# Even block of a two-part transformer: shorter mixing of attention pairs, norm in pieces, cosine products on GpSimd, keys and values of the second softmax later

## The reference, cut to what matters

```python
def diff_attention(q, k, v, lam, subln, lambda_init):      # 4 heads, each a pair of softmaxes
    s = einsum('bqhcd,bkhcd->bhcqk', q, k) * scale
    p = masked_softmax(s, mask)                            # chunk-causal mask
    w = p[:, :, 0] - lam * p[:, :, 1]                      # the pair is mixed
    o = einsum('bhqk,bkhe->bqhe', w, v)                    # 128 values for each head
    return rmsnorm(o, subln) * (1.0 - lambda_init)         # norm over each head's 128 values

def dsa_attention(q, k, v, qi, ki, wi, topk):              # 8 heads of 64
    score = sum over 8 index heads of relu(qi @ ki) * wi
    keep the 64 best keys of each row                      # topk = 64
    p = softmax of q @ k * scale over these; return p @ v

even_mixer = concat(diff_attention, dsa_attention) @ w_out # q and k of both get rotary embedding
```

## Time and profile before

| what | us |
|---|---|
| median of three runs | 1515.05 (1514.8 to 1518.71) |
| the profiled execution, its own time | 1513.2 |
| its span in the trace | 1511.4 |
| TensorE busy in the span | 1441.9 (95%) |
| VectorE busy | 923.5 (61%) |
| ScalarE busy | 746.5 (49%) |
| GpSimd busy | 77.6 (5%) |

### The profile page before, as it was taken

How to read it: one execution, slowest core, us unless ns; L and a number is a source line. 1 busy time by engine, 2 the same in 40 slices (tenths; PEclk the granted TensorE clock), 3 DMA queues, 4 the chain that set the end, 5 groups by cost and what they waited for, 6 DMA issues and landing times.

```text
span 1511.4 us, 17972 instructions
## 1 busy us (share of the span) xinstructions
PE 1441.9 (95%) x6775; PEld 1179.4 (78%) x6775; DVE 923.5 (61%) x1118; ACT 746.5 (49%) x1019; POOL 77.6 (5%) x129
## 2 busy tenths in 40 slices
PE   5999998999999999999889999999999999999998
PEld 4878876778877888877667888878888777778886
DVE  5587775778776554477946655456554555665543
ACT  4556735646546444355446534445344455564442
POOL 3011100000000000031000000000000100000000
PEclk9999999999999999998889999999999999999999
DMA  9786645467554655353214755538555463366550
GB/s 353 271 301 217 205 149 162 166 234 244 191 167 153 223 195 182 129 181 112 100 39 154 263 183 195 187 106 266 180 194 190 124 195 112 112 228 203 195 167 29
DMA packets 177446, 274.29 MB, mean 181 GB/s; under 512 B 6449, under 2 KB 120881, under 8 KB 177361
## 3 DMA queue, kind: packets, MB, share of 16 engines
q1 hardware_dynamic: 170656, 250.87, 49.7%
q0 software_dynamic: 5552, 20.20, 4.3%
q10 hardware_dynamic: 1153, 2.07, 0.4%
HBM read 272.05 MB, written 1.06 MB: 181 GB/s over the span
## 4 chain that ended last, share of the span: by engine, by line
PE 66%; DVE 9%; issue 3%; ACT 2%; DMA 2%; POOL 0%; SPq 0%; DVEq 0%; POOLq 0%; ACTq 0%
PE psum L2189 20%; PE psum L2191 20%; PE psum L2190 20%; DVE w_lo L1810 3%; DMA raw<-in_w_up_dram 2%; DVE PR L2128 2%; PE psum L2390 2%; ACT w_hi L1616 1%; PE psum L2319 1%; PE psum L2318 1%; PE psum L2265 1%; DVE scr L2151 1%; PE psum L2334 1%; DVE lo_at L1810 1%; PE psum L2280 0%
## 5 line engine op out<-in xcount | busy, mean ns | idle before, releaser
L1810 DVE TENSOR_TENSOR w_lo<-raw,w_hi 128x2048 fp32r<-128x2048 f32 (+1 forms) x158 | 358.6, 2273 | 183.6 <-ACT w_hi L1616 183.0
L2189 PE MATMUL psum<-w_hi,hT_hi 128*128 128x512 f32 x1000 | 403.4, 403 | 18.9 <-DVE w_lo L1810 8.5
L2191 PE MATMUL psum<-w_hi,hT_lo 128*128 128x512 f32 x1000 | 393.1, 393 | 0.0
L2190 PE MATMUL psum<-w_lo,hT_hi 128*128 128x512 f32 x1000 | 392.9, 393 | 0.0
L1616 ACT ACTIVATE w_hi<-raw 128x2048 fp32r<-128x2048 f32 (+1 forms) x158 | 299.6, 1899 | 136.7 <-PE psum L2191 91.8
L2189 PEld LDWEIGHTS psum<-w_hi,hT_hi 128*128 128x128 f32 x1000 | 190.8, 191 | 67.4 <-issue 20.9
L2191 PEld LDWEIGHTS psum<-w_hi,hT_lo 128*128 128x128 f32 x1000 | 190.1, 190 | 41.1
L2190 PEld LDWEIGHTS psum<-w_lo,hT_hi 128*128 128x128 f32 x1000 | 190.7, 191 | 37.1 <-issue 0.5
L1810 DVE TENSOR_TENSOR lo_qk<-raw,hi_qk 128x2048 fp32r<-128x2048 f32 (+1 forms) x35 | 79.2, 2264 | 41.2 <-ACT hi_qk L1616 41.2
L2189 PE MATMUL psum<-w_hi,hc_hi 128*128 128x512 f32 x256 | 100.5, 393 | 1.8 <-DVE hc_lo L1815 1.1
L1810 DVE TENSOR_TENSOR lo_at<-raw,hi_at 128x2048 fp32r<-128x2048 f32 x35 | 80.1, 2290 | 35.8 <-ACT hi_at L1616 35.8
(11 more groups left out here) (210 smaller groups left out, 2064.2 us busy)
## 6 DMA issues: line engine op xcount, KB each, us to landing
raw<-in_ffn_wg_dram SPq DMA_DIRECT2D x88, 512.0 KB, 3.7
raw<-in_ffn_wu_dram SPq DMA_DIRECT2D x88, 512.0 KB, 4.7
raw<-in_ffn_wd_dram SPq DMA_DIRECT2D x44, 1024.0 KB, 4.9
raw<-in_w_up_dram SPq DMA_DIRECT2D x44, 512.0 KB, 5.1
raw<-in_w_in_dram SPq DMA_DIRECT2D x19, 1024.0 KB, 7.4
ada_raw<-in_w_ada_dram POOLq DMA_DIRECT2D x24, 512.0 KB, 5.1
raw<-in_even_w_in_dram SPq DMA_DIRECT2D x12, 1024.0 KB, 5.0
raw<-in_odd_w_in_dram SPq DMA_DIRECT2D x12, 1024.0 KB, 5.2
```

Of the source, the lines that this page charges most:

```text
L1810: nc.vector.tensor_tensor(lo_of(s), raw_of(s), hi_of(s).bitcast(F32), ALU.subtract).then_inc(lo_ready, 1)
L2189: nc.tensor.matmul(o, a_hi, b_hi, start=start, stop=False)
L2190: nc.tensor.matmul(o, a_hi, b_lo, start=False, stop=False)
L2191: return nc.tensor.matmul(o, a_lo, b_hi, start=False, stop=stop)
```

## The change

Five things are done in the even block.

1. **Mixing.** Before, both probabilities of a pair were scaled (two operations each) and added. Now the second alone is scaled, by lambda times the first's sum over the second's sum, and added to the unscaled first. The factor that is left, one over the first's sum, is applied to the output in `diffout`.
2. **diffout** works in pieces of one head: for each of 2 row tiles and 4 heads a scaled square with its sum (128 columns), and a scaled copy. That is 16 operations of ScalarE in place of 4.
3. **Norm in pieces.** The sums of squares on VectorE are gone. `diffvar` (one small operation) stands in step 1 of the second softmax, `diffnorm` is four operations of 128 columns for a row tile, one tile in step 2 and one in step 3.
4. **Cosine products on GpSimd** for `bq` and `bk`: four products of 128x512 on GpSimd for each, and VectorE only adds.
5. **Fillers moved.** `first_of(4)` and `second_of` go from steps 3, 4 to steps 5, 6, the rotary embedding of `bk` from step 5 to step 7, `fill_turn` of `bq` from 5 to 4; the projection of the values, `first_of(5)` and `second_of`, goes from steps 6, 8 of the first softmax to steps 0, 1 of the second; `turn_first` and `out_first` stand one step earlier.

```diff
             fills = [[first_of(3), topk(0)], [second_of, topk(1)], [topk(2), rope_of(3, "bq")],
-                     [first_of(4), topk(3)], [second_of, topk(4)],
-                     [fill_turn(3, "bq", 8), topk(5), rope_of(4, "bk")],
-                     [topk(6), first_of(5)], [topk(7)], [second_of], [fill_turn(4, "bk", 12)]]
+                     [topk(3)], [fill_turn(3, "bq", 8), topk(4)],
+                     [first_of(4), topk(5)],
+                     [second_of, topk(6)], [topk(7), rope_of(4, "bk")], [], [fill_turn(4, "bk", 12)]]
...
-            fills = [[], [lambda: pl.add("diffnorm", uses=o_diff, st=sd, v=v, n=sd["n"])], [], [], [],
-                     [turn_first("scr", ("scr_ready", v))], [out_first(W["even_w_out"][0])]]
+            fills = [[first_of(5)], [second_of, diff_var], [diff_norm(0)], [diff_norm(1)], [turn_first("scr", ("scr_ready", v))],
+                     [out_first(W["even_w_out"][0])]]
...
                         ins = nc.gpsimd.tensor_tensor(o, sw, sn, ALU.mult)
+                        if a["by_pool"]:
+                            xs = pr[:, t, c0:c0 + w].rearrange("p (h d) -> p h d", h=nh)
+                            cs = tab[:, t, 0:dim][:, None, :].to_broadcast([P, nh, dim])
+                            mark(ins)
+                            ins = nc.gpsimd.tensor_tensor(scr[:, t, 0:w].rearrange("p (h d) -> p h d", h=nh), xs, cs,
+                                                          ALU.mult)
...
-                        nc.scalar.activation(scr[:, t, BANK:D], psum[:, use.bank, :], ACT.Square)
-                        nc.scalar.activation(scr[:, t, 0:BANK], psum[:, use.bank, :], ACT.Copy)\
-                            .then_inc(psum_read[use.bank], 1)
+                        for h in range(4):
+                            o, r = psum[:, use.bank, h * P:(h + 1) * P], rsum[:, a["n0"] + 2 * h, t:t + 1]
+                            if h:
+                                act.wait_ge(act_step, done)
+                            done = mark(nc.scalar.activation(junk[:, t, 0:P], o, ACT.Square, scale=r,
+                                                             accum_out=col(a["st"], "ss", 4 * t + h)))
+                            ins = nc.scalar.activation(scr[:, t, h * P:(h + 1) * P], o, ACT.Copy, scale=r)
...
-                    for t in range(TT):
+                    for t in range(0 if a["by_pool"] else TT):
...
-                    link(nc.vector.reciprocal(rsum[:, n_ - 1:n_ + 1, :], sums[:, n_ - 1:n_ + 1, :]))
-                    link(nc.vector.tensor_scalar(rsum[:, n_, :], rsum[:, n_, :], lam[:, 2:3], None, ALU.mult))
+                    link(nc.vector.reciprocal(rsum[:, n_, :], sums[:, n_, :]))
+                    link(nc.vector.scalar_tensor_tensor(rsum[:, n_, :], rsum[:, n_, :], lam[:, 2:3], sums[:, n_ - 1, :],
+                                                        ALU.mult, ALU.mult))
                     for t, (b, e) in enumerate(((0, P), (P, SC))):
-                        m = mark(nc.vector.tensor_scalar(prob[:, n_ % 4, b:e], prob[:, n_ % 4, b:e], rsum[:, n_, t:t + 1],
-                                                         None, ALU.mult))
-                    dve.wait_ge(dve_step, m)
-                    for t, (b, e) in enumerate(((0, P), (P, SC))):
-                        ins = nc.vector.scalar_tensor_tensor(prob[:, (n_ - 1) % 4, b:e], prob[:, (n_ - 1) % 4, b:e],
-                                                             rsum[:, n_ - 1, t:t + 1], prob[:, n_ % 4, b:e],
+                        ins = nc.vector.scalar_tensor_tensor(prob[:, (n_ - 1) % 4, b:e], prob[:, n_ % 4, b:e],
+                                                             rsum[:, n_, t:t + 1], prob[:, (n_ - 1) % 4, b:e],
                                                              ALU.mult, ALU.add)
```

More of the change, by code:

```diff
@@ L1157, in go @@
                 def go():
-                    held[name] = rope(pl, i * BANK, 8, HD, held[i])
+                    held[name] = rope(pl, i * BANK, 8, HD, held[i], by_pool=True)
                 return go
@@ L1173, in build_plan, with diff_var, diff_norm @@
             sd = pl.new_stat(8)
-            pl.add("diffout", uses=o, st=sd)
+            pl.add("diffout", uses=o, st=sd, n0=n0)
             v = scr_version()
-            sd["n"] = pl.var()
-            fills = [[], [lambda: pl.add("diffnorm", uses=o_diff, st=sd, v=v, n=sd["n"])], [], [], [],
-                     [turn_first("scr", ("scr_ready", v))], [out_first(W["even_w_out"][0])]]
+            def diff_var():
+                sd["n"] = pl.var()
+                pl.add("diffvar", uses=o_diff, st=sd, n=sd["n"])
+            def diff_norm(t):
+                return lambda: pl.add("diffnorm", t=t, st=sd, n=sd["n"])
+            fills = [[first_of(5)], [second_of, diff_var], [diff_norm(0)], [diff_norm(1)], [turn_first("scr", ("scr_ready", v))],
+                     [out_first(W["even_w_out"][0])]]
             o_diff = o
@@ L1217, in build_plan, with rope @@
     return pl
-def rope(pl, col, heads, dim, uses, replicate=False):
+def rope(pl, col, heads, dim, uses, replicate=False, by_pool=False):
     n = pl.ropes
     pl.ropes = n + 1
-    pl.add("rope", col=col, heads=heads, dim=dim, uses=uses, replicate=replicate, i=n)
+    pl.add("rope", col=col, heads=heads, dim=dim, uses=uses, replicate=replicate, by_pool=by_pool, i=n)
     return n + 1
@@ L1557, in _ @@
                         ins = nc.gpsimd.tensor_tensor(o, sw, sn, ALU.mult)
+                        if a["by_pool"]:
[4 more added lines that the diff above has]
+                                                          ALU.mult)
+                        if t == 0:
+                            mark(ins)
                     ins.then_inc(rope_swapped, 1)
-                elif kind in ("var", "diffnorm"):
+                elif kind in ("var", "diffvar"):
                     st, n_ = a["st"], a["n"]
@@ L1676, in _ @@
                 elif kind == "diffout":
+                    act.wait_ge(first_scale_ready, 1)
                     for t in range(TT):
@@ L2010, in _ @@
                     ins.then_inc(mixed_ready, 1)
+                    if n_ == 15:
+                        nc.vector.reciprocal(rsum[:, 8:16:2, :], sums[:, 8:16:2, :]).then_inc(first_scale_ready, 1)
                 elif kind == "oevac":
@@ L2031, in _ @@
                             wait_read(dve, use)
-                elif kind == "diffnorm":
-                    st = a["st"]
-                    for t in range(TT):
-                        wait_read(dve, a["uses"][t])
-                        s0 = st["ss"][0] + 4 * t
-                        m = mark(nc.vector.tensor_reduce(stat[:, s0:s0 + 4],
-                                                         scr[:, t, BANK:D].rearrange("p (h d) -> p h d", h=4), AX.X,
-                                                         ALU.add))
-                    dve.wait_ge(dve_step, m)
-                    nc.vector.tensor_scalar(stat[:, st["v"][0]:st["v"][1]], stat[:, st["ss"][0]:st["ss"][1]],
-                                            1.0 / (2 * HD), EPS, ALU.mult, ALU.add).then_inc(var_ready, 1)
-                    dve.wait_ge(rstd_ready, a["n"])
-                    for t in range(TT):
-                        o = scr[:, t, 0:BANK].rearrange("p (h d) -> p h d", h=4)
-                        r0 = st["r"][0] + 4 * t
-                        link(nc.vector.tensor_tensor(o, o, stat[:, r0:r0 + 4][:, :, None].to_broadcast([P, 4, P]),
-                                                     ALU.mult))
-                        ins = nc.vector.scalar_tensor_tensor(o, o, 1.0 - LAMBDA_INIT,
-                                                             subln[:, None, :].to_broadcast([P, 4, P]), ALU.mult, ALU.mult)
-                        if t == 0:
-                            link(ins)
-                    ins.then_inc(scr_ready, 1)
-                    dve.wait_ge(scr_ready, a["v"])
@@ new lines, in _ @@
+                elif kind == "diffvar":
+                    st, k = a["st"], 1.0 / (1.0 - LAMBDA_INIT) ** 2
+                    for use in a["uses"]:
+                        wait_read(dve, use)
+                    nc.vector.tensor_scalar(stat[:, st["v"][0]:st["v"][1]], stat[:, st["ss"][0]:st["ss"][1]],
+                                            k / (2 * HD), k * EPS, ALU.mult, ALU.add).then_inc(var_ready, 1)
+                elif kind == "diffnorm":
+                    t = a["t"]
+                    dve.wait_ge(rstd_ready, a["n"])
+                    for h in range(4):
+                        o = scr[:, t, h * P:(h + 1) * P]
+                        ins = nc.vector.scalar_tensor_tensor(o, o, col(a["st"], "r", 4 * t + h), subln[:, :], ALU.mult,
+                                                             ALU.mult)
+                        if (t, h) == (1, 3):
+                            ins.then_inc(scr_ready, 1)
+                        else:
+                            m = mark(ins)
+                    if t == 0:
```

(1 more changed line is left out.)

4 lines of the change are left out of this document (added).

## The result

| | kernel before | changed kernel |
|---|---|---|
| median, 22 runs each | 1514.46 us (1508.74 to 1520.02) | 1518.2 us (1514.24 to 1522.1) |
| ratio, 95% interval | | 1.0032 (1.002 to 1.0043) |
| profiled execution, its span | 1513.2, 1511.4 | 1520.41, 1518.6 |
| head 2's to head 15's logits on VectorE | 71.53 | 77.10 |

What follows compares the result with a forecast made beforehand. It took VectorE as the bound from 713 to 746 us, TensorE in its place after the change; step by step head 15 came at 786.9 against 785.02, +1.9, 1517.0 us against the median, range 1510.5 to 1523.5.

Steps and rivals of the forecast that it cites:

- Its case, no change with TensorE in VectorE's place: Heads 2 to 15: TensorE bounds where VectorE did, 1511.5 to 1519.6 us; chance 57%.
- The sum of +1.9: Head 15's logits at 786.9 against 785.02, taken as the change of the whole kernel's time.
- rotation of `bq` on GpSimd, VectorE's wait: Ahead of the add of `bq`: four GpSimd products take 5.2 us and VectorE waits 3.1 us.
- small work up to `first_of(4)` at the half clock: TensorE's transposes, logits, turns, values and logits after idling: 7.35 us at the half clock, 4.0 at the full.
- 0.7 for the first few at the half clock (between 0 and 1.4): Slow start of `first_of(4)` ahead of head 6: 0.7 us added to its 5.45.
- its sister of 0.8: Slow start of the values' projection ahead of head 10: 0.8 us added to 5.45.
- the first rival: TensorE's clock stays low into the products: 4.8 us each, 1521 at one place, 1525 at both; chance 20%.
- the third rival: GpSimd is blocked: a rotation could take 12.9 us, 7.7 more at each of two places, 1525 to 1532; chance 6%.
- The 0.5 for a held-up GpSimd: Rotation of `bk`: the search's closing operations on VectorE may hold GpSimd up, between nothing and 0.9 us; 0.5 taken.
- `diffout` at nothing: ScalarE's 16 operations, bound at 6.2 us, cost nothing because 13.4 us of products cover them.
- The second rival: VectorE bounds and its shed 11.0 us, less GpSimd waits of 3.1 and 1.1, give 6.8: 1508; chance 17%.
- The values' projection as a loss: Ahead of head 10: products and logits of 13.4 us make it 3.35 us late, gained back in part.

Runs made afterwards that it cites:

- e5: Changed kernel with 34 and 19 idle matmuls in TensorE's two idle stretches; ratio 0.9988 to the kernel before.
- e12: e5 with the cosine products back on VectorE and 28 and 17 idle matmuls; ratio 0.9971 to the kernel before.
- e1: Kernel before with the changed arithmetic alone: old order of the fillers, cosine products on VectorE; ratio 0.999 to the kernel before.
- e6: e1 with 13 idle matmuls in TensorE's 3.15 us wait for ScalarE behind head 10's logits; ratio 0.9938 to the kernel before.
- e8: e1 with the values' projection in steps 0 and 1 of the second softmax, turn_first and out_first one step earlier; ratio 0.9974 to the kernel before.
- e7: e1 with the last 24 matmuls of the values' projection cut in two, 12 moved behind head 9's logits; ratio 0.9948 to the kernel before.
- e11: e8 with 5 and 13 idle matmuls in the waits for the second and third mixing; ratio 0.9999 to the kernel before.

## Why the prediction was right, and which terms were off

Its case, no change with TensorE in VectorE's place, is what happened, and the median of 1518.2 lies within the case's own 1511.5 to 1519.6. Against the kernel before, the ratio makes the change 4.8 us, 0.32%, just over what I called no change (4.5 us); the medians make it 3.7, inside. The sum of +1.9 was too small: by 1.8 us by the medians, 2.9 by the ratio, 3.7 by the trace. By its steps, the changed kernel's times less 1.78:

| step | forecast | trace |
|---|---|---|
| rotation of `bq` on GpSimd, VectorE's wait | 5.2, 3.1 | 4.9, 3.02 |
| mixing to the next logits | 1.15 | 1.13 |
| head 3 | 721.75 | 721.54 |
| small work up to `first_of(4)` at the half clock | 7.35 | 7.14 |
| head 5 | 729.3 | 729.0 |
| `first_of(4)` | 5.45 + 0.7 | 7.4 |
| head 6 | 736.7 | 737.6 |
| head 7 | 743.8 | 744.8 |
| add of `bk` ends | 750.4 | 751.4 |
| small work up to `first_of(5)` | 6.3 | 6.3 |
| head 8 | 756.8 | 758.0 |
| `first_of(5)` | 5.45 + 0.8 | 8.2 |
| head 10 | 770.2 | 773.6 |
| head 15 | 786.9 | 790.6 |

**The step that failed** is "0.7 for the first few at the half clock (between 0 and 1.4)", and its sister of 0.8. They are 1.9 and 2.8: behind a first matmul of 0.59 us, eight of the first product and twelve of the second stood 0.43 us apart. With them go 1.2 and 2.0 of the 3.7 us; 0.3 lies behind head 10. It is the mechanism of the first rival, which had 20% and priced it at 4.8 for each place if the whole product was slow; what came was about half of that, at both places. Its two parts, an idle stretch and then small work at 1.2 GHz, were seen, but the size of the slow start was a guess, and the trace of before had it. Three products there begin slow, at 722.78, 735.62 and 746.36; they last 6.9, 7.2 and 7.0 us to the next work, 1.4 to 1.7 over the 5.45, so 0.7 was too little by every one of them. Of the second, the first two and the last of its slow matmuls, and the first at the full clock:

```profile
735.62 0.66 PE L2189 MATMUL psum<-w_hi,hT_hi 128*128 128x512 f32 x1
736.07 0.63 PE L2190 MATMUL psum<-w_lo,hT_hi 128*128 128x512 f32 x1
...
739.06 0.47 PE L2191 MATMUL psum<-w_hi,hT_lo 128*128 128x512 f32 x1
739.36 0.39 PE L2189 MATMUL psum<-w_hi,hT_hi 128*128 128x512 f32 x1
```

Two smaller slips are in the same terms: a product at the full clock takes 5.6 us and not 5.45 (5.58 and 5.67 in e5's trace), and 719.15 with 2.53 is 721.68, not 721.75. e5 prices the half clock as a whole: with these waits filled and nothing else changed, 6.7 us come out, small work and slow starts together.

**The mixing, the norm.** 1.13 for the mixing is the forecast's. Four pieces of the norm took 1.13 us, 0.28 each and not 0.22, 0.5 us more for all eight. They stood ahead of `turn_first`, for which TensorE waited 1.17 us.

**GpSimd.** The rotations took 4.9 and 5.1 us as forecast, and no split fell beside them, so the third rival did not come. The 0.5 for a held-up GpSimd was not needed: it was VectorE that was held. Its two closing operations took 2.80 us where I had 0.9 for both; the add began at 751.96, 0.45 after GpSimd's last product ended, and the rest it would have waited anyway. Together the two rotations on GpSimd cost 1.75 us up to head 8 (e12) and 2.0 to 2.6 us by the ratios.

**`diffout` at nothing** was right for this order, on the condition that the prediction gave for it: it ended at 762.3 under `first_of(5)`. In e1, without that cover, TensorE waited 3.15 us, and filling it gave 7.9 (e6).

**The second rival**, that what VectorE sheds comes out, gave 6.8 us. Its 11.0 us were a little low: the four cosine products had taken 1.78 and 1.42 us in the trace of before, 3.2 and not 2.6. In this order it does not, even at the full clock: e12, the same without GpSimd's waits, is at 0.9971, 4.4 us. In the old order with the clock held, e6, 9.4 us come out.

**The values' projection as a loss** was wrong. I counted it as 13.4 us ahead of head 10 (15.6 in the trace, with the slow start), gained back in part. In the changed kernel's trace the clock is full behind it and `diffout` is covered, so that heads 10 to 15 need 17.0 us where e1's need 24.3 (and e6's, with the clock held, 17.1). e8 comes out level with e1 or below it.

What stays open: why the clock falls behind one short wait and not behind another. The same 0.58 us wait for ScalarE stands in slow and in fast stretches. e1 and e6 are the same up to head 10, and yet the clock fell behind e1's wait for the second mixing and not behind e6's:

```profile
734.66 0.70 PE L2353 MATMUL psum<-cst,attn 128*128 128x128 f32 x3 [2.08 <-DVE attn L2026]
```

```profile
731.26 0.52 PE L2356 MATMUL psum<-cst,attn 128*128 128x128 f32 x3 [2.09 <-DVE attn L2029]
```

Likewise TensorE waited 1.17 or 1.18 us ahead of `turn_first` in the changed kernel, e5 and e12, and only e5's clock fell. So the length of such a wait does not decide it, and what one trace shows there need not come in the next execution. With the kernel before, the place of its short slow stretches is not the changed kernel's either. No series of kernels here shortened one wait step by step.

## What to carry to other kernels

Price a wait of TensorE by the work that stands behind it, not by its own length: here filling 8.4 and 4.6 us of waiting gave 6.7 us in what followed. Count the slow matmuls in the trace that you have before you put a price on a slow start. When work is taken off the engine that bounds a stretch, keep TensorE's long products where its waits are: here the order with a product beside the other engine's longest chain won in all three pairs, and half a product in a 3 us wait gave 6.4 us (e7). If no real work fits, idle matmuls in the wait are worth trying, and must be measured each time, since two of the five kernels that had them gained nothing: the slow stretch had moved to a worse place.

## What the runs showed of the hardware that I had not expected

GpSimd beside VectorE, in the changed kernel:

```profile
746.42 1.30 POOL L1565 TENSOR_TENSOR scr<-PR,cst 128x512 f32<-128x512 f32 x1 [25.75 <-ACT PR L1726]
...
748.92 1.25 POOL L1565 TENSOR_TENSOR scr<-PR,cst 128x512 f32<-128x512 f32 x1
750.14 1.37 POOL L1570 TENSOR_TENSOR scr<-PR,cst 128x512 f32<-128x512 f32 x1
```

GpSimd kept its 1.25 to 1.37 us while VectorE's closing operations, L1988 and L1989 above, each took about as long as the product of GpSimd that they met. L1988 has one tensor as input. In e12, with GpSimd idle, the same two were:

```profile
739.32 0.36 DVE L1991 TENSOR_SCALAR work<-work 128x384 f32<-128x384 f32 x1
739.71 0.56 DVE L1992 SCALAR_TENSOR_TENSOR selbias<-work,cst 128x384 f32<-128x384 f32 x1
740.31 1.42 DVE L1958 TENSOR_TENSOR scr<-PR,cst 128x512 f32<-128x512 f32 x2
```

I had expected a wait of two-input operations only. The Trainium skill, "SBUF — State Buffer", section "Who interferes with whom", says that a `tensor_scalar` can also take the shared port pair; the 0.36 to 1.30 us agree. The last row is the pair of cosine products on VectorE: 1.42 us, where the four products on GpSimd take 5.1 in place of its own two.

The place decides what idle matmuls do: 13 of them, 3.17 us, were worth 7.9 us at one place (e6), and 18 at two others gave nothing and came out 3.8 over (e11).
